# The sixteen u tiles of the gated mixer in two partial sums: one wide product per weight tile, VectorE adds the parts, ScalarE's gelu in place

## The reference

```python
def chunked_sgu_mixer(x, w_in, ln_g, ln_b, w_s, b_s, w_out):
    z = jax.nn.gelu(x @ w_in, approximate=False)      # 256 x 1024 @ 1024 x 4096
    u, v = jnp.split(z, 2, axis=-1)                   # 2048 columns each
    v = layer_norm(v, ln_g, ln_b)
    ...
    mixed = jnp.einsum('gts,bnsgc->bntgc', w, v) + b_s.T[None, None, :, :, None]
    return (u * mixed.reshape(B, S, SGU_HALF)) @ w_out
```

## Time and profile before

| | us |
|---|---|
| three runs, median | 1348.73 |
| span of the profiled execution, first to last instruction | 1347.0 |
| TensorE products busy in the span | 1336.4 |
| VectorE busy | 1043.8 |
| ScalarE busy | 657.3 |
| GpSimd busy | 76.9 |

### The profile page before, as it was taken

One profiled execution on the slowest core, in us unless ns is written; L12 is line 12 of the kernel. 1 busy time (PEld: TensorE's weight loads), 2 busy tenths in 40 slices (PEclk: granted clock), 3 DMA queues, 4 the chain that ended last, 5 costly groups with the idle time before them and its releaser, 6 DMA issues.

```text
span 1347.0 us, 21379 instructions
## 1 busy us (share of the span) xinstructions
PE 1336.4 (99%) x8305; PEld 1199.3 (89%) x8305; DVE 1043.8 (77%) x1538; ACT 657.3 (49%) x824; POOL 76.9 (6%) x87
## 2 busy tenths in 40 slices
PE   9999999999999999999999999999999999999997
PEld 7999988888899999899889999889999887899996
DVE  8879697777877778669987778767777878777777
ACT  6667544333444344554353434444444478643433
POOL 0000150000000000100020000100000100200001
PEclk9999999999999999999999999999999999999999
DMA  9543647776567767565566656766656540466651
GB/s 335 161 155 119 242 158 226 233 244 213 192 219 252 264 208 243 187 192 186 174 215 209 207 198 231 245 212 227 210 189 216 163 157 30 164 228 205 209 197 63
DMA packets 183741, 268.64 MB, mean 199 GB/s; under 512 B 5917, under 2 KB 148673, under 8 KB 183408
## 3 DMA queue, kind: packets, MB, share of 16 engines
q1 hardware_dynamic: 178510, 249.95, 56.1%
q0 software_dynamic: 4368, 16.44, 3.6%
q10 hardware_dynamic: 786, 1.18, 0.4%
HBM read 262.32 MB, written 4.19 MB: 198 GB/s over the span
## 4 chain that ended last, share of the span: by engine, by line
PE 98%; DVE 1%; DMA 0%; ACT 0%; SPq 0%; issue 0%; POOL 0%; POOLq 0%; DVEq 0%
PE bank L920 95%; PE bank L943 3%; DMA ring<-in_w_in 0%; DVE stats L2478 0%; DVE resid L2473 0%; ACT split L1934 0%; DVE resid L3254 0%; ACT xn L1943 0%; SPq L740 0%; ACT sd L1875 0%; DVE resid L2506 0%; DVE resid L2519 0%; POOL resid L3407 0%; POOLq L395 0%; DVE resid L3249 0%
## 5 line engine op out<-in xcount | busy, mean ns | idle before, releaser
L920 PE MATMUL bank<-hT,split 128*128 128x256 f32 (+2 forms) x4472 | 672.9, 311 | 0.0
L920 PEld LDWEIGHTS bank<-hT,split 128*128 128x128 f32 (+1 forms) x4472 | 626.6, 191 | 47.9 <-issue 3.3
L1865 ACT ACTIVATE split<-ring 128x2048 fp32r<-128x2048 f32 (+1 forms) x220 | 420.6, 1914 | 467.1 <-PE bank L920 460.6
L2426 DVE TENSOR_TENSOR split<-ring,split 128x2048 fp32r<-128x2048 f32 x216 | 492.5, 2281 | 177.8 <-ACT split L1865 176.8
L920 PE MATMUL bank<-split,hid_hi 128*128 128x512 f32 x992 | 271.3, 380 | 0.0
L920 PEld LDWEIGHTS bank<-split,hid_hi 128*128 128x128 f32 x992 | 183.1, 189 | 23.8 <-issue 0.3
L920 PE MATMUL bank<-split,hT 128*128 128x512 f32 (+1 forms) x744 | 167.9, 379 | 0.2 <-ACT split L1934 0.2
L920 PEld LDWEIGHTS bank<-split,hT 128*128 128x128 f32 x744 | 134.6, 190 | 21.3 <-issue 3.8
L920 PE MATMUL bank<-split,hid_lo 128*128 128x512 f32 x496 | 151.4, 379 | 0.0
L2796 DVE TENSOR_REDUCE act_out<-bank 128x256 f32<-128x512 f32 x188 | 128.7, 686 | 23.2 <-PE bank L920 22.7
L920 PEld LDWEIGHTS bank<-split,hid_lo 128*128 128x128 f32 x496 | 93.7, 189 | 13.2
(11 more groups left out here) (253 smaller groups left out, 889.4 us busy)
## 6 DMA issues: line engine op xcount, KB each, us to landing
ring<-in_ffn_w SPq DMA_DIRECT2D x126, 1024.0 KB, 5.1
ring<-in_w_in SPq DMA_DIRECT2D x17, 1024.0 KB, 5.2
ring<-in_w_mlp_in SPq DMA_DIRECT2D x16, 1024.0 KB, 6.1
ring<-in_w_mlp_out SPq DMA_DIRECT2D x16, 1024.0 KB, 4.8
ring<-in_sgu_w_in SPq DMA_DIRECT2D x16, 1024.0 KB, 5.4
ring<-in_sgu_w_out SPq DMA_DIRECT2D x8, 1024.0 KB, 4.7
ring<-in_ffn_w SPq DMA_DIRECT2D x12, 512.0 KB, 4.5
ring<-in_w_out SPq DMA_DIRECT2D x4, 1024.0 KB, 4.8
```

Of the source, the lines that this page charges most:

```text
L920: ins = pe.matmul(o, lhsT, rhs, start=start, stop=stop)
L1865: act.activation(halves(q if i is None else q + BODY, n)[0], ring[:, u % SLOTS, 0:n], ACT.Copy).then_inc(hi_ready, 1)
L2426: dve.tensor_tensor(lo, ring[:, u % SLOTS, 0:n], hi.bitcast(F32), ALU.subtract).then_inc(split_ready, 1)
```

## The change

Each u tile is made by `up_T_parts` in the whole bank. VectorE adds the two parts into `uT` (`add_u`), which frees the bank. ScalarE's gelu then works in place on `uT`, two tiles per unit, one unit late and after the rounding of the next unit, and signals `u_ready`. The adds are placed by hand in VectorE's order.

```diff
@@ TensorE
-                    up_T_split(o[:, 0:S], parts(("su", i), KT), f * P, P).then_inc(tile_done, 1)
+                    up_T_parts(o, parts(("su", i), KT), f * P).then_inc(tile_done, 1)
@@ ScalarE
+            def gelu_u(ft):
+                tile_copied(act, ("su", ft))
+                act.activation(uT[:, ft, :], uT[:, ft, :], ACT.Gelu).then_inc(u_ready, 1)
             for i in range(8):
-                for f in range(2):
-                    o = tile_ready(act, ("su", 2 * i + f))
-                    act.activation(in_order(uT[:, 2 * i + f, :]), from_streams(o[:, 0:S]), ACT.Gelu).then_inc(frees(("su", 2 * i + f)), 1)
                 round_unit(mixer[i + 11])
+                if i:
+                    for f in range(2):
+                        gelu_u(2 * i - 2 + f)
                 if i == 1:
...
+            for ft in range(14, 16):
+                gelu_u(ft)
@@ VectorE
+            def add_u(i):
+                for ft in (2 * i, 2 * i + 1):
+                    o = tile_ready(dve, ("su", ft))
+                    add_parts(uT[:, ft, :], o).then_inc(frees(("su", ft)), 1)
             v_stats(0)
             low_unit(mixer[11])
             v_stats(1)
+            add_u(0)
             low_unit(mixer[12])
             dve.wait_ge(sgu_in, 16 * 4)
             rest_units = mixer[13:19]
...
                 link(dve.tensor_scalar(vtok[:, b, :], vtok[:, b, :], mv[:, b, 0:1], rstd[:, b:b + 1],
                                        ALU.subtract, ALU.mult))
-                if rest_units:
-                    low_unit(rest_units.pop(0))
+                add_u(1 + 2 * b)
+                low_unit(rest_units.pop(0))
                 link(dve.tensor_tensor(vtok[:, b, :], vtok[:, b, :], sgu_g, ALU.mult))
-                if rest_units:
-                    low_unit(rest_units.pop(0))
+                add_u(2 + 2 * b)
+                low_unit(rest_units.pop(0))
                 dve.tensor_tensor(vtok[:, b, :], vtok[:, b, :], sgu_b, ALU.add).then_inc(v_ready, 1)
+            add_u(5)
             low_unit(rest_units.pop(0))
+            for i in range(6, 8):
+                add_u(i)
@@ gated
-                    tile_copied(dve, ("su", ft))
+                    dve.wait_ge(u_ready, ft + 1)
```

More of the change, by code:

```diff
@@ L601, in two_blocks @@
         k_swapped = [sem(f"k_swapped{i}") for i in range(4)]
+        u_ready = sem("u_ready")
         cx_ready = sem("cx_ready")
```

## The result

The changed kernel takes 1370.99 us (median of 5 runs, 1370.72 to 1371.73) against 1348.73 of the kernel before: 22.3 us longer, ratio 1.0165 with a 95% interval from 1.0154 to 1.0176. I had forecast 1359.8 in a range up to 1365.0. The direction was right and the loss twice as large.

A forecast was written before the change was run, and what follows sets the result against it. TensorE's products were taken to bound the kernel. New TensorE waits of 12.1 us less 1.0 saved give 11.1; 1348.7 + 11.1 = 1359.8 us, range 1355.0 to 1365.0 at 0.8.

The forecast's parts named there:

- What bounds the kernel: Whole kernel: TensorE's products, busy 1336.4 of 1347.0 us; a change costs whatever it makes TensorE wait.
- the additions exceed VectorE's room: Mixer's u stage: 9.8 us of new VectorE work against 4.2 us of idle time before the first gated value.
- the bookkeeping: VectorE's order in the u stage written out with durations, checked on the old order; output product starts 11.1 us later.
- The products, 1.0 us: TensorE's u tiles: 2.62 us each instead of 2.68, gaining 1.0 us on the path; bounds 0 and 2.0.
- The additions, 0.61 us each: VectorE's sixteen new additions: 0.61 us from start to start, other bound 0.72; 9.8 us, up to 11.5.
- ScalarE's gelu in place, nothing on the path: ScalarE's gelu moves from PSUM to SBUF, 0.386 to 0.407 us each: 0.3 us, on an engine with 17 us free.
- u5 so ends at 602.5; ScalarE can round su5 only then: u stage, after u4's bank wait: su5 is rounded to 604.6, and VectorE, done at 602.7, waits 1.9 us.
- TensorE's use of the unit three back: ScalarE's queue: what releases a rounding; VectorE being late by less than that release costs nothing.
- The clock's rival: TensorE's clock falls in the new waits: +12.8 to about +16, so 1361.5 to 1365 us; chance 0.32.
- The later cycle stays 6.06: After the first output product, a unit keeps taking TensorE 6.06 us; nothing more lost or won back.
- the ring of waits: u stage: the rounding waits for TensorE, and TensorE for VectorE; given as argument against the milder meeting.
- a milder case: VectorE's lateness counts only as work less idle time: 5.6 to 8 us, 1354.3 to 1357; chance 0.11.

The follow-up runs named there:

- experiment 2: Changed kernel with the u tiles over eight PSUM banks instead of four; 1355.39 us, ratio 1.0047.
- experiment 5: Changed kernel with only VectorE's order altered: additions of units 0 to 6 each one low half or norm pass earlier; 1355.94 us, ratio 1.0052.
- experiment 3: Kernel before with the wide products alone, the addition of the two partial sums left out; 1348.25 us, ratio 0.9993.
- experiment 8: Changed kernel with eight banks and each addition made twice, first into rows nobody reads; 1365.80 us, ratio 1.0123.
- experiment 1: Changed kernel with each su unit's release on a small product right behind the unit's own last tile; 1362.02 us, ratio 1.0097.
- experiment 4: Changed kernel with eight further 512-column products ahead of six u tiles, filling TensorE's waits; 1370.55 us, ratio 1.0161.
- experiment 6: On experiment 5, last u tile added behind the first gated pair, GpSimd doing v's norm gain and shift for block 0 and half of block 1; 1359.03 us.
- experiment 7: As experiment 6, but with all four passes of v's norm gain and shift on GpSimd; 1359.64 us, ratio 1.0086.

## Why the prediction was right and wrong

- **What bounds the kernel, and that the additions exceed VectorE's room: right.** 9.8 us of new work against 4.2 of idle time is about what experiments 2 and 5 are left with: +6.2 and +7.5, for 6.0 and 5.6 by the bookkeeping, and in both profiled runs the clock falls once on the path, for 1.5 to 1.7 us.
- **The products, 1.0 us:** 2.62 us a tile as read in the feed-forward; the path to the output product 0.84 us shorter (experiment 3). The spacing of the Trainium skill (TensorE: Matmul & The Clock Gate, Back-to-back issue gap), which that section calls the one of an isolated product, gives as an estimate a gain of 0.3 us; the trace stands further from it than from my 1.0.
- **The additions, 0.61 us each:** right. 0.60 on the path by the traces of experiments 8 and 2, 0.65 by the medians. But a bank comes free later than I had it: u10 starts 621.65 - 620.81 = 0.84 us after the addition that frees its bank, and I had 0.61 + 0.06.
- **ScalarE's gelu in place, nothing on the path:** right for the work. The roundings wait for TensorE and not behind a gelu.
- **The step that failed:** "u5 so ends at 602.5; ScalarE can round su5 only then", and before it the sentence that a rounding's own release is "TensorE's use of the unit three back". The release is not the end of the use, which was the mistake. It rides on the first product of the next tile, and my rounding times stood wherever that product was the one waiting. My check of the bookkeeping against the old order could not find this: there the next product comes at once, and both readings give the same times to 0.1 us. Experiment 1, which makes the step true, measures +12.9 for my +11.1. With the step corrected the sum is +19.8.
- **The rest, 22.3 less 19.8 = 2.5:** some 1.7 us is the fallen clock, 1.4 over u15 and the mix tile ahead of it and 0.3 at u8 (experiment 4 beside the changed kernel). For the last 0.8 no run was made. The rows show small things that recur in every unit and are of its size: the 0.84 us just named where I had 0.67, and the rounding 0.55 us after the first product where the corrected bookkeeping has 0.48. The rounding behind u14's first product comes 0.83 us after it, with the granted clock at 1.00; why stays open.
- **The clock's rival:** it happened, and I priced four falls too high (about +16 less 11.1, for some 1.7 measured), since three of the four lay where TensorE had to wait anyway. As the cause of the miss it is out: filling the waits returned 0.4 us by the medians, 0.9 against the kernels before, and the clock's 1.7 us is small beside the 11.2 missed.
- **"The later cycle stays 6.06":** right; from 651.85 the output products run as before, and nothing is lost or won there.
- **The range:** its upper end came from the clock. It had no case for a lateness that feeds itself, though the prediction named the ring of waits (rounding for TensorE, TensorE for VectorE) as the argument against a milder case.

No version beats the kernel before. At most 0.84 us can be won, and every way tried to pay for sixteen additions costs 6 us or more. No run gave some of VectorE's work to ScalarE, which was busy only 22.0 of 39.0 us in this stage.

## What to carry to other kernels

Before a step is delayed, look for what is posted late with it: a release that rides on the next instruction is as late as that instruction's own waits. A schedule worked out should be tested on a case where the two readings of a dependency differ, not only on the old order. And when a wait closes a ring through three engines, its price is paid once per turn, so ways to open it (here an earlier release, more banks, an earlier read) are the first things to try. An idle engine is no free help before one has looked at what it shares with the busy one.

## What the runs showed of the hardware that I had not expected

A VectorE instruction with two SBUF inputs, 128 x 2048, takes up to 5.5 us in place of 2.28 while GpSimd works on SBUF, and once 6.68; one that reads PSUM is not slowed (1.27 us the pair). In all twelve overlaps of experiments 6 and 7 the instruction that began later ended as if it had stood still until the earlier was done: VectorE's 128 x 2048 instruction 2.14 to 2.15 us after GpSimd's pass, GpSimd's of that size 4.4 us after VectorE's, and the two of 128 x 1024 1.08 and 2.20 us after. The Trainium skill, GPSIMD Engine Reference, Key points, says that the two share SBUF interfaces and contend where VectorE has two SBUF inputs. The trace agrees with this.

That TensorE's granted clock could fall in such waits was a rival; that single waits of 2.4 to 2.7 us, with dense products on both sides, do it four times in 50 us is more than I had thought. The length of the wait alone does not decide it in these runs. In the changed kernel a wait of 2.26 us before u14 left the granted clock at 1.00. In experiment 1 one of 2.35 us left it at 1.00 (596 to 602 us), and one of 2.05 was followed by 0.50 (610 to 613 us).
